# Block 2's gate and up products computed by token halves for 12 of 16 column blocks, with the first net's modulation tiles, sums and value blocks rescheduled

## The reference, cut to what matters

```python
# block 1, its feed-forward part (D_FF = 5632)
u = causal_dwconv3(h @ w_up, ffn_conv_w)          # 2048 -> 11264, three taps over tokens
g, val = jnp.split(u, 2, axis=-1)
y = (silu(g) * val) @ w_down                      # 5632 -> 2048
# modulation of both blocks: silu(c) @ w_mod + b_mod, a matrix-vector product, 2048 x 12288
# block 2, its mixing part
proj = h @ w_in                                   # pool, q, k, v, g_a, g_b
y_a = multiscale_pool(u_pool, ...) @ w_a_up       # 1024 -> 2048
y_b = stick_breaking_attention(q, k, v) @ w_b_up  # 1024 -> 2048
merged = sigmoid(g_a) * y_a + sigmoid(g_b) * y_b
x = x + gate1 * (merged @ w_o)
```

## Time and profile before

| | |
|---|---|
| median of 3 runs | 2472.98 us (2472.69 to 2473.2) |
| the profiled execution, its own time | 2473.39 us |
| its span in the profile | 2471.7 us |
| granted TensorE clock over the span | 1.00 |
| PE busy | 98% of the span |
| DVE busy | 77% |
| ACT busy | 49% |
| HBM read | 647.58 MB |

### The profile page before, as it was taken

The page is one execution under the profiler, slowest core; times in us unless marked ns, Lnnn a source line. Parts: engine busy times, 40 slices in busy tenths (PEclk is TensorE's granted clock), DMA queues, the critical chain, the costliest instruction groups (busy, mean ns, idle before and its releaser), DMA issues.

```text
span 2471.7 us, 34060 instructions
## 1 busy us (share of the span) xinstructions
PE 2433.2 (98%) x13372; PEld 2107.6 (85%) x13376; DVE 1908.5 (77%) x2287; ACT 1220.0 (49%) x1592; POOL 383.9 (16%) x669
## 2 busy tenths in 40 slices
PE   7899999999999999999999999999999999999999
PEld 4699999988888888879988888888998888888887
DVE  6879999969976887889968688998777645545555
ACT  4354545545554544545545566554455544435433
POOL 0000000014412412443000000000003402203214
PEclk9999999999999999999999999999999999999999
DMA  9988898678987888988559677987679856656665
GB/s 382 408 349 307 325 357 325 221 256 291 293 285 256 296 295 293 293 269 289 187 197 330 230 288 259 325 320 289 205 250 342 286 200 207 209 199 207 209 206 162
DMA packets 242050, 673.43 MB, mean 272 GB/s; under 512 B 23345, under 2 KB 66353, under 8 KB 201697
## 3 DMA queue, kind: packets, MB, share of 16 engines
q1 hardware_dynamic: 219794, 645.06, 74.1%
q0 software_dynamic: 21664, 24.85, 3.8%
q10 hardware_dynamic: 432, 1.35, 0.2%
HBM read 647.58 MB, written 2.10 MB: 263 GB/s over the span
## 4 chain that ended last, share of the span: by engine, by line
PE 91%; DMA 4%; DVE 3%; issue 1%; ACT 1%; POOL 0%; SPq 0%; DVEq 0%; ACTq 0%
PE PS L845 15%; PE PS L847 15%; PE PS L846 15%; PE PM L707 12%; PE PM L710 6%; PE PM L694 5%; PE PM L695 5%; PE PM L696 5%; DMA raw<-in_w_mod 3%; PE PS L745 2%; PE PS L741 2%; PE PS L742 2%; DVE WL L1516 1%; PE PM L760 1%; PE PS L797 1%
## 5 line engine op out<-in xcount | busy, mean ns | idle before, releaser
L1516 DVE TENSOR_TENSOR WL<-raw,WH 128x1024 fp32r<-128x1024 f32 (+2 forms) x841 | 993.7, 1200 | 451.5 <-ACT WH L1097 449.9
L1097 ACT CAST WH<-raw 128x1024 fp32r<-128x1024 f32 (+2 forms) x841 | 859.4, 1032 | 901.7 <-PE PS L847 572.7
L1523 DVE CUSTOM_DVE_ANT_0 raw<-raw,cb 128x2048 f32<-128x2048 f32 x192 | 438.1, 2282 | 19.4 <-DMA raw<-in_w_mod 17.3
L845 PE MATMUL PS<-WH,H 128*128 128x512 f32 x992 | 386.1, 389 | 0.0
L847 PE MATMUL PS<-WH,H 128*128 128x512 f32 x992 | 385.9, 389 | 0.0
L846 PE MATMUL PS<-WL,H 128*128 128x512 f32 x992 | 385.9, 389 | 0.0
L2094 POOL DMA_DIRECT2D UR<-tmps x320 | 184.4, 584 | 702.0 <-DVE tmps L1629 674.2
L2094 POOL DMA_DIRECT2D FD<-TU x208 | 119.8, 584 | 953.5 <-DVE TU L1737 938.2
L707 PE MATMUL PM<-H,WH 128*128 128x512 f32 x832 | 262.4, 397 | 0.1
L845 PEld LDWEIGHTS PS<-WH,H 128*128 128x128 f32 x992 | 186.2, 188 | 38.8
L846 PEld LDWEIGHTS PS<-WL,H 128*128 128x128 f32 x992 | 186.2, 188 | 38.6
(11 more groups left out here) (384 smaller groups left out, 4176.4 us busy)
## 6 DMA issues: line engine op xcount, KB each, us to landing
raw<-in_w_ff SPq DMA_DIRECT2D x128, 1024.0 KB, 5.1
raw<-in_w_in SPq DMA_DIRECT2D x110, 1024.0 KB, 6.3
raw<-in_w_mod SPq DMA_DIRECT2D x96, 1024.0 KB, 7.0
raw<-in_w_ada SPq DMA_DIRECT2D x96, 1024.0 KB, 5.7
raw<-in_w_up SPq DMA_DIRECT2D x80, 1024.0 KB, 6.1
raw<-in_w_down SPq DMA_DIRECT2D x24, 1024.0 KB, 6.6
raw<-in_w_out SPq DMA_DIRECT2D x16, 1024.0 KB, 5.8
raw<-in_w_o SPq DMA_DIRECT2D x16, 1024.0 KB, 5.5
```

Of the source, the lines that this page charges most:

```text
L845: PE.matmul(b, hi, WH[:, u % NUNIT, w], start=(k + q == 0), stop=False)
L1097: S.copy(part(WH), w).then_inc(s_hi, 1)
L1516: V.tensor_tensor(part(WL), w, part(WH).bitcast(F32), ALU.subtract).then_inc(s_lo, 1)
L1523: V.tensor_tensor_reduce(w, w, cb[:, :], 1.0, 0.0, ALU.mult, ALU.add, mods[:, which, tile:tile + 1]).then_inc(s_mod, 1)
```

## The change

Twelve of the 16 column blocks of `w_a_up`, `g_a`, `g_b` and `w_b_up` become three jobs of four blocks each, by tokens (`aupt`, `gat`, `gbt`, `bupt`). Blocks 12 to 15 stay by features. The number of loads, units and slots is as before (447 loads, 841 units, 445 slots). Each of these token jobs uses two of the four `PM` banks, (1, 2) or (3, 0). Its loads take 2 or 4 steps of 128 rows out of four column blocks. ACT copies `aupt`'s result to `MF` (which is `M` seen as four flat pieces), applies the sigmoid straight from PSUM for `gat` and `gbt`; DVE multiplies and adds 1024 elements at a time, transposes the merged piece into the new buffer `TM`, and POOL carries it back into `M`; ACT and DVE make the two parts six and seven slots later.

In the first net: the value blocks start one slot later (lag 6 to 10 in place of 5 to 9); `TURNED1` and its waits swap the first two buffers, so that block 0 goes to `UF[0]` behind `s_gc` and block 1 to `TT` behind `s_tb`; and the 48 modulation tiles of these stages are placed anew.

Modulation tiles by stage, before and after (from `MODS_AT`): up 1 to 4: 13, 9; down 0: 3, 7 (all in its first seven slots); up 5 to 7: 8, 6; down 1: 5, 11 (one in each of its first eleven slots); up 8 to 10: 11, 8; down 2: 5, 7; down 3: 3, 0. No other stage's number differs.

```diff
+J_AUP = (jobs_of("aupt", "w_a_up_2", range(2), 8) + jobs_of("aup", "w_a_up_2", range(12, 16), 8)
+         + jobs_of("aupt", "w_a_up_2", [2], 8))
+J_GA = ([Job("gat", f, ("w_in_2", 8 + f), 16) for f in range(3)]
+        + [Job("ga", i, ("w_in_2", 32 + i), 16) for i in range(12, 16)])
+J_GB = ([j for f in range(3) for j in (Job("gbt", f, ("w_in_2", 12 + f), 16), Job("bupt", f, ("w_b_up_2", f), 8))]
+        + [j for i in range(12, 16) for j in (Job("gb", i, ("w_in_2", 48 + i), 16), Job("bup", i, ("w_b_up_2", i), 8))])
...
+MERGED = {n: (1, 2) if (j.kind, j.i) in (("aupt", 0), ("aupt", 2), ("gat", 1)) or j.kind == "gbt" else (3, 0)
+          for n, j in enumerate(JOBS) if j.kind in ("aupt", "gat", "gbt", "bupt")}
...
-STREAM += spread(L_FFN[0:40], mod_tiles(0, 80)) + spread(L_FFN[40:48], [])
-STREAM += spread(L_FFN[48:124], mod_tiles(1, 16, 0)) + spread(L_FFN[124:] + O_PROJ, [])
+_mm80, _mm2a = mod_tiles(0, 80), mod_tiles(1, 16, 0)
+STREAM += spread(L_FFN[0:32], _mm80[0:8]) + spread(L_FFN[32:40], _mm80[8:]) + spread(L_FFN[40:48], [])
+STREAM += spread(L_FFN[48:68], _mm2a[0:6]) + spread(L_FFN[68:80], _mm2a[6:17]) + spread(L_FFN[80:104], _mm2a[17:25])
+STREAM += spread(L_FFN[104:116], _mm2a[25:]) + spread(L_FFN[116:] + O_PROJ, [])
...
+            TM = sb("TM", [128, 1024], on=mix2)
...
-        TURNED1 = [TT, UF[0], UF[1], ug[:, :, :].rearrange("p a t -> p (a t)")]
+        TURNED1 = [UF[0], TT, UF[1], ug[:, :, :].rearrange("p a t -> p (a t)")]
...
+            def wait_merged(n):
+                j = JOBS[n]
+                if (j.kind, j.i) in (("aupt", 0), ("aupt", 1), ("aupt", 2), ("gat", 0), ("gbt", 0), ("bupt", 0)):
+                    for b in MERGED[n]:
+                        PE.wait_ge(s_taken[b], sum(1 for q in BANK_OF if q < n and BANK_OF[q] == b))
+                elif j.kind == "gat":
+                    PE.wait_ge(*((s_tau, 3), (s_tga, 1))[j.i - 1])
+                elif j.kind == "gbt":
+                    PE.wait_ge(s_tgb, j.i)
+                else:
+                    PE.wait_ge(s_tbp, j.i)
...
-                elif j.kind == "upt" and j.i >= 11 and 5 <= lag < 10:
-                    for q, part in ((lag - 6, "high"), (lag - 5, "scale")):
+                elif j.kind == "upt" and j.i >= 11 and 6 <= lag < 11:
+                    for q, part in ((lag - 7, "high"), (lag - 6, "scale")):
...
+                elif j.kind in ("gat", "gbt") and lag == 1:
+                    S.wait_ge(s_unit, JOB_ENDS[n])
+                    if j.i:
+                        S.wait_ge(s_tgp if j.kind == "gat" else s_tbm, j.i)
+                    elif j.kind == "gbt":
+                        S.wait_ge(s_gap, 2)
+                    for half in range(2):
+                        ins = S.activation(gate[:, half * 512:(half + 1) * 512], token_half(n, half), ACT.Sigmoid)
+                    ins.then_inc(s_tga if j.kind == "gat" else s_tgb, 1)
+                elif j.kind == "bupt" and lag == 6:
+                    S.wait_ge(s_mb, 256 * (j.i + 1))
+                    S.copy(MG[:, 4 * j.i:4 * j.i + 4, 0:T], M[:, 4 * j.i:4 * j.i + 4, :]).then_inc(s_mht, 1)
...
-                        V.wait_ge(*((s_tb, 256 * 20), (s_gc, 40), (s_up, 40), (s_up, 40))[j.i])
+                        V.wait_ge(*((s_gc, 40), (s_tb, 256 * 20), (s_up, 40), (s_up, 40))[j.i])
...
+                elif j.kind == "bupt" and lag == 1:
+                    V.wait_ge(s_unit, JOB_ENDS[n])
+                    V.wait_ge(s_tgb, j.i + 1)
+                    for half in range(2):
+                        z = gate[:, half * 512:(half + 1) * 512]
+                        ins = V.tensor_tensor(z, z, token_half(n, half), ALU.mult)
+                    ins.then_inc(s_tbp, 1)
+                    V.wait_ge(s_tbp, j.i + 1)
+                    V.wait_ge(s_tgp, j.i + 1)
+                    V.tensor_tensor(MF[j.i], MF[j.i], gate, ALU.add).then_inc(s_tbm, 1)
+                    V.wait_ge(s_tbm, j.i + 1)
+                    if j.i:
+                        V.wait_ge(s_mb, 256 * j.i)
+                    for half in range(2):
+                        ins = V.transpose(turned(TM[:, :])[:, half, :, :, :], half_rows(MF[j.i], half))
+                    ins.then_inc(s_mt, 1)
...
+            for f in range(3):
+                G.wait_ge(s_mt, f + 1)
+                carry(MF[f], TM[:, :], s_mb)
```

More of the change, by code:

```diff
@@ L113 @@
 for _n in range(len(JOBS)):
-    if _n not in OPENING and _n not in BY_TOKENS and JOBS[_n].kind not in ("qk", "v"):
+    if _n not in OPENING and _n not in TOKENS and JOBS[_n].kind not in ("qk", "v"):
         BANK_OF[_n], USE_OF[_n] = _count % NBANK, _count // NBANK
@@ L425, in build @@
         S0, S2, S3, S23 = PS[0][:, 0:T], PS[0][:, 2 * T:3 * T], PS[0][:, 3 * T:4 * T], PS[0][:, 2 * T:4 * T]
+        MF = [M[:, 4 * f:4 * f + 4, :].rearrange("p a t -> p (a t)") for f in range(4)]
+        gate = gt[:, :, :].rearrange("p a t -> p (a t)")
         TT = tmps[:, :, :].rearrange("p a t -> p (a t)")
@@ L580, in low, with token_half @@
             return tmps[:, BANK_OF[n], :]
-        def token_half(m, half):
+        def token_half(n, half):
+            if n in MERGED:
+                return PM[MERGED[n][half]][:, :]
+            m = BY_TOKENS[n]
             if m < 2:
@@ L829, in run_tokens @@
                             PE.wait_ge(s_f2, 16 * j.g + kk - 7)
+                if j.kind in ("aupt", "bupt") and j.i == 0:
+                    for kk in range(k, k + nk):
+                        PE.wait_ge(s_ya if j.kind == "aupt" else s_yb, kk + 1)
                 if j.kind == "downt" and j.i == 0:
@@ L841, in run_tokens @@
                         else:
-                            rows = FB[j.g % 2][:, k + q, :] if j.kind == "downt" else H[:, k + q, :]
+                            if j.kind == "downt":
+                                rows = FB[j.g % 2][:, k + q, :]
+                            else:
+                                rows = YAB[:, k + q, :] if j.kind in ("aupt", "bupt") else H[:, k + q, :]
                             hi, lo = (rows[:, c + half * 128:c + half * 128 + 128] for c in (0, T))
@@ L1680, in behind @@
                         take(n, K2[:, j.i - 16, :])
+                elif j.kind == "gat" and lag == 2:
+                    V.wait_ge(s_tau, j.i + 1)
+                    V.wait_ge(s_tga, j.i + 1)
+                    V.tensor_tensor(MF[j.i], MF[j.i], gate, ALU.mult).then_inc(s_tgp, 1)
+                elif j.kind == "bupt" and lag == 1:
[11 more added lines that the diff above has]
+                        V.wait_ge(s_mb, 256 * j.i)
+                    for half in range(2):
+                        ins = V.transpose(turned(TM[:, :])[:, half, :, :, :], half_rows(MF[j.i], half))
+                    ins.then_inc(s_mt, 1)
+                elif j.kind == "bupt" and lag == 7:
+                    V.wait_ge(s_mht, j.i + 1)
+                    m = MG[:, 4 * j.i:4 * j.i + 4, :]
+                    V.tensor_tensor(m[:, :, T:2 * T], M[:, 4 * j.i:4 * j.i + 4, :], m[:, :, 0:T].bitcast(F32),
+                                    ALU.subtract).then_inc(s_mgt, 1)
                 elif j.kind == "aup" and lag == 1:
```

93 lines of the change are left out of this document (60 added, 33 removed).

## The result

The changed kernel takes 2485.80 us in the median of four runs (2483.82 to 2487.68), the kernel before, on the same chip, 2472.84 us (2471.83 to 2473.20). The ratio is 1.0053, 95% interval 1.0036 to 1.0070: slower by 13 us, outside the forecast range of 2465.0 to 2482.5. The profiled execution took 2483.82 us, its span is 2482.5; it is the shortest of the four, so its trace holds 10.8 us of the 13.

The account below looks back on a forecast made before the run. PE, busy 98% of the span, was taken to bound the kernel by matmul time plus gaps. Terms -4.8 - 3.7 + 6.5 + 4.5 = +2.5 us on 2473.39 gave 2475.9, median 2475.5 us; range 2465 to 2482.5.

Parts of the forecast that it names:

- the excess becomes waits on `WL`: Down 0 and 1: DVE work beyond the stage's matmul time makes PE wait, 2.5 and 4.3 us as lower bounds.
- Layout, -4.8 us: Block 2's products by tokens: matmuls start closer together, 0.0083 us less for each of 576 moved tiles, 4.8 us less.
- the 0 for new waits: Block 2's token jobs: DVE's heavy and light turns together need 10.5 of 10.9 us, so no wait; other bound 8 us.
- Swap and later value blocks, -3.7 us: Down 2: DVE's idle of 4.87 us goes; of three PE gaps totalling 4.5 us, 0.8 stays; bounds -4.5 and 0.
- Down 1, +6.5 us: Down 1 with six more tiles: PE waits 6.5 us; bounds 4.3 (DVE alone) and 10 (DMA share).
- down 0, +4.5 us: First 40 us of down 0 with four more tiles: PE waits 4.5 us; bounds 2.5 and 6.
- the 408 GB/s: Most any profiled stretch moved, with every DMA engine full; taken to show that down 1's needed 394 GB/s was possible.
- The ring runs dry: Slower rival, down 0 and 1: ACT, DVE and PE wait for loads, costing 6 and 10 us; 2480.5 us, chance 0.25.
- The down groups swallow the tiles: Faster rival: moved tiles cost nothing in the down groups, leaving -9.3 us; 2463.7 us, chance 0.20.
- the turns of 8.3 us: Rival, mixing part: DVE's `bupt` turns block PE, +8 us, 2483 us; chance 0.07 together with the layout gains nothing.
- the layout gains nothing: Rival, block 2: token spacing is worse on small banks, the 4.8 us are lost, +7.3; shares 0.07 with the turns of 8.3 us.
- 2470 to 2479.5, from its bounds: The forecast's own range without the rivals, said to come from its terms' bounds; a fifth of it over 2477.9 us.

Follow-up runs that it names:

- e4: The kernel before with only block 2's products by tokens (no swap, later value blocks or new tile order): 2473.54 us, ratio 1.0000.
- e1: The changed kernel with the first net's modulation tiles where they were before: 2465.91 us, ratio 0.9969.
- e3: The kernel before with only the swapped sum buffers and the value blocks one slot later: 2468.42 us, ratio 0.9977.
- e5: The changed kernel, DVE summing only 256 of 2048 columns of the 48 moved modulation tiles, loads whole: 2475.14 us, ratio 1.0004.
- e6: The changed kernel, only 256 of 2048 columns of the 48 moved modulation tiles loaded, DVE's work whole: 2478.96 us, ratio 1.0021.
- e11: e1 with 8 modulation tiles in down group 1, between 5 and 11: 2470.92 us, ratio 0.9990.
- e2: The kernel before with only the new placement of the 48 modulation tiles: 2485.23 us, ratio 1.0047.
- e12: The kernel before with only the value blocks one slot later: 2473.59 us, ratio 1.0002.

## Why the prediction was wrong

The forecast was 2475.5 us, the result 2485.8. No single term makes the 10.3 us: on the profiled spans down 0 and down 1 together cost 3.5 us more than forecast, down 2 cost 2.7 more and the layout gave 2.5 less, and the median lies 2.0 us above the profiled execution. What the first two have in common is the step "the excess becomes waits on `WL`": DVE's work over the stage's matmul time was taken for the price, in down 0 and 1 with a part on top, in down 2 alone. The wait that ends last is another one, ACT's for loads that SP could issue only behind DVE's sums. Step by step:

**Layout, -4.8 us.** The spacing is right: 0.227 us on the small banks. What came of it in the trace is -2.9 us up to the first `wo`, since the gap of 2.17 us stands in `gat`. By the medians it is 0.0 (e4 against before) and -2.5 us (e1 against e3). Mis-sized by 2 to 5 us: the closer spacing holds, the 0 for new waits doesn't. I had looked for a block in `bupt`'s turn and had counted DVE's total in 1536 to 1674 us; the gap came in an earlier stretch, from tiles that the change did not move, and the later ones from loads that land late. That the 48 small carries make these loads late is not shown: no kernel was run without them.

**Swap and later value blocks, -3.7 us.** The mechanism is right (the idle of 4.87 us and all three gaps go in e3), its size alone is 4.9 us. In the changed kernel 3.5 us are lost in down 2, not 0.8, from the same loop as in down 1: ACT waits 23.0 us for loads there. The term took 60.3 us of DVE work for 60.0 us of matmuls and so almost no wait. How much of the 3.5 us the two added tiles make, and how much the places of the others, no run separates.

**Down 1, +6.5 us, and down 0, +4.5 us.** Lost are 8.4 and 6.1 us: for down 1 inside my bounds, for down 0 just over the upper one, and above what I took in both. Here the prediction failed first, at the sentence "I take 6.5, nearer to the DVE rows, since the 408 was really reached". Two things are wrong in it. First, the 408 GB/s belong to another mix. In down 0 of e5 full DMA engines gave 346 GB/s. The rule that I set aside, 358 GB/s for a core (the Trainium skill, "DMA: Bandwidth & Descriptors", Specifications), is nearer to this stage than the row that I set against it. That doesn't make it a ceiling, stand. Another page of the Trainium skill ("Perfetto Trace Analysis", Roofline, under Engine Utilization) lets one active core pull more than its share; the 408 GB/s agree. Second, I took DVE's excess and the ring's as alternatives of which the larger bounds the stage. They are links of one loop: SP can't refill a buffer before DVE has summed it, the load lands 7.4 us after issue (median of `w_down`'s 1 MB loads in 872 to 940 us, 6.7 before), and DVE then waits with idle that it can't make good. e5 and e6 show that each alone costs PE time, e11 that the cost begins before DVE is full. The loop itself is read from traces: no run changed the number of raw buffers or put the tiles' loads behind the weights' in the queue, which would test it directly.

**The rivals.** *The ring runs dry* gave the mechanism and most of the amount: 16 us for down 0 and 1 together, 14.5 measured. Its 2480.5 us is 5.3 short for what it left out: down 2 (2.7 more), the layout (2.5 more), and a median 2.0 us above the profiled execution; that it priced down 0 and 1 at 1.5 too much goes the other way. *The down groups swallow the tiles* is refuted by e2. Of *the turns of 8.3 us* and *the layout gains nothing* the second came partly true in its amount (the 4.8 us are lost in e4), but not by its reason: the spacing is as close as forecast. The first has the number nearest to the result, 2483 us, by luck: PE has no gap in 1536 to 1674 us of the changed kernel, where `bupt`'s turns lie.

**The range.** "2470 to 2479.5, from its bounds" doesn't follow from the bounds. With all three upper ones (0 for down 2, +10, +6) and the -4.8 the sum is +11.2, 2484.2 us, above the 2482.5 at which the whole range ended; the upper ends were treated as if they could not meet. They nearly did.

**The sum again.** On the spans, the forecast was +2.5; down 1 adds 1.9, down 0 1.6, down 2 2.7, and the layout, at -2.3, 2.5; 0.6 goes off since the kernel before had lost 5.1 us and not 4.5: +10.6 against 10.8 measured.

**What stays open.** Why executions of one kernel differ by up to 8 us by tokens; and whether the 2 us between this profile and the median are stretches at 1.2 GHz as in e4. The granted clocks fit that: 0.999 in the two executions of 2483.8 and 2483.9 us, 0.997 in the two of 2487.7. But e5's longest, 2478.43 us, has 0.999 too. The best version is e1, the change without its new order of tiles: 7.4 us less than before, 19.9 less than the change.

## What to carry to other kernels

Where tiles share a ring of buffers and an in-order queue with the weights, don't price an added tile by the excess of the fullest engine. Follow one buffer through its turn (issue, landing, first reader, last reader, next issue) and compare that with the time in which the ring's entries are used: here 11.8 us against 10.9. That is what these traces suggest; as a way to forecast it has not been tried. Read how many GB/s full DMA engines give in the stage itself, and try parts of an edit in pairs: the swap was worth 2.6 us, the lag nothing, both 4.9, and the third part lost more than all gave.

## What the hardware showed that I had not expected

- A gap of PE of about 2 us is in some executions followed by a stretch at 1.2 GHz that costs 1.6 us more. Of 14 gaps of 2.0 to 3.1 us in streams of 512-column matmuls, in the traces of all kernels here, four were: 2.3 us in e2 (down 0, granted clock 0.79 in 712 to 720 us), 2.16 in e4, 2.05 in e5 and 2.15 in e6. Ten were not, among them the longest, 3.1 us in e12, and the 2.17 us in the changed kernel's profile: 0.227 to 0.24 us from start to start behind 1501.64.
- The rate at full DMA share is not one number: 408 GB/s in 24 to 84 us, 346 in down 0 of e5. Which part of the mix (POOL's carry, the sizes of the packets) makes the difference is not shown.
